# Attention heads: exponentials, normalisation, key scaling and rotary additions issued one or two pumps later

## The reference, cut to what matters

```python
proj = rmsnorm(h) @ w_in                     # q, k, v of the neighbourhood heads; cq, ckv, k_pe of the latent ones
# neighbourhood heads (128 wide): q, k normed per head
s = q @ k.T * scale + bias + mask            # a grid of 64 columns, a window of 16, plus the meta tokens
out_a = softmax(s) @ v
# latent heads (128 + 64 rotary)
q = rmsnorm(cq) @ w_q_up ; k, v = rmsnorm(ckv) @ w_kv_up
q, k = rmsnorm(q), rmsnorm(k) ; rotary on the last 64 columns of each
out_b = softmax(q @ k.T * scale) @ v
h = h + concat(rmsnorm(out_a), rmsnorm(out_b)) @ w_out
h = h + conv_glu(rmsnorm(h))                 # then a second block: recurrence, convolution, gated MLP
```

## Time and profile before

| | |
|---|---|
| median of three runs | 2751.41 us |
| the profiled execution | 2753.61 us |
| its span | 2752.2 us |
| TensorE busy | 2677.2 us (97%), 22052 matmuls |
| VectorE busy | 1836.5 us (67%) |
| ScalarE busy | 1248.1 us (45%) |
| GpSimd busy | 324.8 us (12%) |
| attention of the first block | about 100 to 410 us of the span |

### The profile page before, as it was taken

How to read it: one execution, slowest core, us unless ns; L and a number is a source line. 1 busy time by engine, 2 the same in 40 slices (tenths; PEclk the granted TensorE clock), 3 DMA queues, 4 the chain that set the end, 5 groups by cost and what they waited for, 6 DMA issues and landing times.

```text
span 2752.2 us, 51365 instructions
## 1 busy us (share of the span) xinstructions
PE 2677.2 (97%) x22052; PEld 2636.4 (96%) x22052; DVE 1836.5 (67%) x2578; ACT 1248.1 (45%) x1943; POOL 324.8 (12%) x526
## 2 busy tenths in 40 slices
PE   6999999899999999998999999999989999999998
PEld 6988889899999999998999999999989999999998
DVE  5656568777777777776888667766876445454444
ACT  5556555544433444445434443334544433344443
POOL 1110101111111111221000001111221000000001
PEclk9999999999999999999999999999999999999999
DMA  6433445688888888885444568886767556555553
GB/s 200 120 117 94 125 144 176 202 271 263 271 280 283 268 272 273 266 283 177 142 152 153 185 228 270 276 271 218 256 204 252 184 179 189 193 190 184 184 182 125
DMA packets 500084, 571.22 MB, mean 208 GB/s; under 512 B 26704, under 2 KB 473424, under 8 KB 499856
## 3 DMA queue, kind: packets, MB, share of 16 engines
q1 hardware_dynamic: 467968, 463.76, 51.9%
q0 software_dynamic: 31600, 103.80, 11.6%
q10 hardware_dynamic: 288, 0.36, 0.0%
HBM read 565.77 MB, written 2.54 MB: 206 GB/s over the span
## 4 chain that ended last, share of the span: by engine, by line
PE 86%; DVE 7%; ACT 4%; issue 1%; DMA 0%; POOL 0%; SPq 0%; DVEq 0%; ACTq 0%
PE ps L681 27%; PE ps L682 27%; PE ps L683 26%; DVE wl L1780 3%; ACT wh L1273 2%; PE ps L976 1%; PE ps L810 1%; DVE lr L1976 1%; DVE nx L1884 0%; ACT lp L1446 0%; DMA raw<-in_w_in 0%; PE ps L783 0%; DVE sqt L1884 0%; PE ps L835 0%; PE ps L836 0%
## 5 line engine op out<-in xcount | busy, mean ns | idle before, releaser
L1780 DVE TENSOR_TENSOR wl<-raw,wh 128x1024 fp32r<-128x1024 f32 (+1 forms) x894 | 1058.5, 1200 | 630.4 <-ACT wh L1273 626.2
L681 PE MATMUL ps<-xx,wh 128*128 128x256 f32 (+2 forms) x4848 | 1385.8, 286 | 29.2 <-DVE xx L1861 16.3
L682 PE MATMUL ps<-xx,wh 128*128 128x256 f32 (+2 forms) x4848 | 1366.4, 282 | 0.0
L683 PE MATMUL ps<-xx,wl 128*128 128x256 f32 (+2 forms) x4848 | 1363.1, 281 | 0.0
L1273 ACT ACTIVATE wh<-raw 128x1024 fp32r<-128x1024 f32 (+1 forms) x894 | 882.2, 1029 | 621.8 <-PE ps L683 612.3
L681 PEld LDWEIGHTS ps<-xx,wh 128*128 128x128 f32 x4848 | 918.0, 189 | 38.4 <-DVE wl L1780 21.9
L682 PEld LDWEIGHTS ps<-xx,wh 128*128 128x128 f32 x4848 | 918.9, 190 | 1.7 <-issue 1.0
L683 PEld LDWEIGHTS ps<-xx,wl 128*128 128x128 f32 x4848 | 918.4, 189 | 0.0
L681 PE MATMUL ps<-hid,wh 128*128 128x256 f32 x1408 | 393.9, 280 | 0.0
L682 PE MATMUL ps<-hid,wh 128*128 128x256 f32 x1408 | 393.7, 280 | 0.0
L683 PE MATMUL ps<-hid,wl 128*128 128x256 f32 x1408 | 392.8, 279 | 0.0
(11 more groups left out here) (366 smaller groups left out, 2387.4 us busy)
## 6 DMA issues: line engine op xcount, KB each, us to landing
raw<-in_w_in SPq DMA_DIRECT2D x118, 1024.0 KB, 5.3
ada_raw<-in_w_ada POOLq DMA_DIRECT2D x384, 256.0 KB, 4.7
raw<-in_w_gate SPq DMA_DIRECT2D x44, 1024.0 KB, 6.4
raw<-in_w_up SPq DMA_DIRECT2D x44, 1024.0 KB, 7.0
raw<-in_w_ffn_gate SPq DMA_DIRECT2D x44, 1024.0 KB, 5.1
raw<-in_w_ffn_up SPq DMA_DIRECT2D x44, 1024.0 KB, 5.6
raw<-in_w_down SPq DMA_DIRECT2D x32, 1024.0 KB, 6.6
raw<-in_w_ffn_down SPq DMA_DIRECT2D x32, 1024.0 KB, 5.5
```

What stands on the lines that cost most here:

```text
L681: pe.matmul(dst, h[:, c, o:o + w], x[:, 0, k, g.t0:g.t1], start=(k == 0), stop=False)
L682: pe.matmul(dst, h[:, c, o:o + w], x[:, 1, k, g.t0:g.t1], start=False, stop=False)
L683: m = pe.matmul(dst, l[:, c, o:o + w], x[:, 0, k, g.t0:g.t1], start=False, stop=end)
L1780: dve.tensor_tensor(wl[i % NS][:, part], raw[i % NR][:, part], wh[i % NS][:, part].bitcast(F32), ALU.subtract).then_inc(s_lo, 1)
```

## The change

In every head's generators on ScalarE and VectorE, pauses are moved: the exponential comes one pump later; reciprocal and row scaling come two pumps later for the first two query blocks and one for the last; the reciprocals of the norms and the key scaling come one pump later for the first head of a pair and two for the second; the rotary additions come one pump later. The pauses behind them are shortened by as much, so each generator's length stays. TensorE's and GpSimd's programs are untouched.

```diff
 scalar: attend
+                    yield from pause(1)
                     act.wait_ge(s_ldve[lane], event(DVE_EV, f"mx{j}", n))
                     act.activation(p_, src, ACT.Exp, bias=cc[0:w, 0:1], scale=sc, accum_out=cc[0:w, 1:2]).then_inc(s_lact[lane], 1)
...
-                    yield from pause(PAUSES[1] if j < 2 else PAUSES[2])
+                    yield from pause((PAUSES[1] if j < 2 else PAUSES[2]) - 1)
 vector: attend
+                    yield from pause(2 if j < 2 else 1)
                     dve.wait_ge(s_lact[lane], event(ACT_EV, f"ex{j}", n))
                     dve.reciprocal(cc[0:w, 2:3], cc[0:w, 1:2]).then_inc(s_ldve[lane], 1)
...
-                    yield from pause(PAUSES[1] if j < 2 else PAUSES[2])
+                    yield from pause(PAUSES[1] - 2 if j < 2 else PAUSES[2] - 1)
 vector: rstds
-            def rstds(lane, ACT_EV, n):
+            def rstds(lane, ACT_EV, n, late):
...
+                yield from pause(late)
                 dve.wait_ge(s_lact[lane], event(ACT_EV, "sk", n))
 vector: mla
-                yield from rstds(lane, MLA_ACT, n)
+                yield from rstds(lane, MLA_ACT, n, 1 + j)
...
-                yield from pause(PAUSES[5])
+                yield from pause(PAUSES[5] - j)
...
-                yield from pause(PAUSES[6])
+                yield from pause(PAUSES[6] - 1)
 vector: na
-                yield from rstds(lane, NA_ACT, n)
+                yield from rstds(lane, NA_ACT, n, 1 + j)
...
-                yield from pause(PAUSES[5])
+                yield from pause(PAUSES[5] - 1 - j)
```

## The result

The changed kernel takes 2770.36 us (median of four runs, 2767.63 to 2772.49), the kernel before 2750.01 beside it: a ratio of 1.0071, 95% interval 1.0059 to 1.0083, so 0.7% slower. The forecast was 2769, slower.

A forecast was written before the change was run, and what follows sets the result against it. TensorE, busy 97% of the span, was taken to bound the kernel. Attention terms of 15.7 us plus 1.6 for the clock gave 17.3, moving the median from 2751.41 to 2768.7, stated as 2769; range 2755 to 2780.

The forecast's parts named there:

- L0: First latent head pair: normalisation falls behind the second half's split, so rows reach TensorE's transposes late; +0.85 us.
- N0: First neighbourhood pair: query eviction gap goes, but the second normalisation comes late behind the next slab's split; +0.5 us.
- L1: Second latent pair: key scaling and rotary additions end behind splits, later than TensorE wants them; +1.15 us.
- N1 with L2: Dense stretch of second neighbourhood and third latent pair: keys, rotary products and normalisations late behind splits; +5.0 us.
- N2 with L3: Stretch of third neighbourhood and fourth latent pair: same lateness pattern, VectorE already late at its start; +3.9 us.
- N3: Last neighbourhood pair: second key scaling and second normalisation late behind out projection evictions and splits; +4.3 us.
- For L0 the same chain ends before its transposes: 0: Step claiming the first latent pair's later key scaling and rotary additions still finish before TensorE's transposes; no added time.
- The clock: More and longer TensorE gaps in attention were to bring one more fall of the granted clock; +1.6 us.
- rival C: Each new TensorE gap brings a clock fall, five more at 1.6 us: 2777; chance 0.10.
- A: Rival: with no split delaying normalisation, the spread order closes TensorE's attention gaps, 10 us: 2741, faster; chance 0.08.
- B: Rival: enough slack after all, sums off by a few tenths each and only moves remain: 2751; chance 0.08.
- D: Rival: later exponentials alternate with the other pair's square roots, adding table loads; 2774 with four unhidden; chance 0.04.

The follow-up runs named there:

- e1: The changed kernel with key scaling and rotary additions back at their old pumps, only exponentials, row reciprocals and row scaling late: 2758.75 us, 1.0031 against the kernel before.
- e3: The kernel before with exponential, reciprocal and row scaling all exactly one pump late, keys and rotary additions as before: 2745.91 us, ratio 0.9986.
- e8: e1 with the second half of slabs of more than two chunks split before pump 2 instead of pump 3, during attention: 2750.92 us, 0.9999 against the kernel before.
- e10: e8 with the normalisation of the last neighbourhood pair (N3) one pump late instead of two: 2746.89 us, ratio 0.9991 against the kernel before.
- e2: The changed kernel with softmax back at its old pumps, only key reciprocals, key scaling and rotary additions late: 2766.05 us, ratio 1.0058 against the kernel before.
- e4: The changed kernel with the second half of every slab, two-chunk ones too, split before pump 2: 2764.39 us, ratio 1.0052 against the kernel before.
- e9: The changed kernel with the second half split before pump 2 only in slabs of more than two chunks: 2762.6 us, 1.0041 against the kernel before.
- e6: The changed kernel with GpSimd's mask addition cut from 128x512 to 128x4 elements: 2766.69 us, ratio 1.0055 against the kernel before.
- e5: The changed kernel with the last neighbourhood pair (N3) alone back on its old pumps: 2764.56 us, ratio 1.0053 against the kernel before.
- e7: e3 with the second half split before pump 2 in slabs of more than two chunks: 2749.2 us, ratio 0.9999 against the kernel before.

## Why the prediction was right, and where it was short

**The bound and the place.** Right: all added idle time lies in attention, and the stretches behind are as long as before. Of the signs listed, VectorE's waits for exponentials did not nearly vanish, 6.8 of 17.7 us are left; the others came.

**The mechanism.** Right. For the softmax half (8.2 us, e1) it is shown: not the later exponential but a split ahead of the normalisation makes it late. e3, e8 and e10 each take it away differently and each get the time back. For the keys and rotary additions (15.5 us, e2), the larger half, it is only in part shown: the early split shortens the waits for the rotary product from 10.5 to 6.1 (e4) and 7.5 us (e9), and the rest is read from the timelines, as in the chain at 249.96. Beside it stand GpSimd's collisions (e6) and a clock loss that rests on one profile each.

**The terms**, in us: once as how far the starts of the same TensorE work part between the two profiles, which has clock falls in it, and once as TensorE's waits for attention results in that stretch, after less before:

| step | forecast | starts part by | waits added |
|---|---|---|---|
| L0 | 0.85 | 2.7 | 1.9 |
| N0 | 0.5 | 1.0 | 0.6 |
| L1 | 1.15 | 2.4 | 1.9 |
| N1 with L2 | 5.0 | 6.1 | 4.0 |
| N2 with L3 | 3.9 | 4.1 | 3.6 |
| N3 | 4.3 | 5.8 | 2.9 |
| sum | 15.7 | 22.1 | 14.9 |

The sum without the clock was right within a microsecond, which is partly luck: the latent pairs L0 and L1 were too small (2.0 for 3.8), the large three too large (13.2 for 10.5), and the errors cancel. (By its own figures N3 was 5.9 less 1.4, 4.5 and not 4.3.) From the first sums of squares of L0 to the last product with v the profile grew by 18.9 us (298.65 to 317.54); the 22.1 count from a little later and leave out a clock fall of 3.2 us at 108 to 116 us that the profile before has and the one after has not. It does not come with the change: of the twelve profiles, the three that reach attention last have it (before, e2 and e3). 18.9 less the difference in clock loss, 3.4, is 15.5: the order again. N3 shows how the two stand together: 2.9 us of waits, 3.4 us of clock loss from 392 to 416 us behind them, and undoing N3 alone (e5, whose profile has no loss there) gave 5.8.

**The step that failed** is "For L0 the same chain ends before its transposes: 0". The rotary product ended 1.69 us late, because GpSimd's mask addition fell on two operations of the chain. With L1 this was 2.6 us (e6), where the sum had none. The Trainium skill (SBUF — State Buffer, section "SBUF: two separate sides") had the rule; my estimate by it, 18.4 instead of 17.3, was nearer and still short, because I applied it to L1 only. The trace agrees with the rule: 1.53 us beside GpSimd, 0.42 without. It does not agree in every row with whichever comes second being the one that is blocked: the split of 4.26 us began 0.6 us before the additions that it waited for, by GpSimd's recorded times, which are rough.

**N0.** The eviction gap went and the wait for the normalised row came in its place, 2.58 us for 2.02: the forecast's +0.5. It came sooner than "2 us later" of the text: at 168.72 it is the same transposes that stood at 173.55, in an execution that was about 5 us ahead.

**The clock.** One more fall was forecast. There were more:

```profile
168.00:172.00 4.00, 3.28 (x17) 3.13 (x18) 2.26 (x7) 3.26 (x10) 0.00 (x0) 0.57 0.27 35
```

At 168.72 six transposes took 1.54 us instead of 0.82 at the lower level (1.2 GHz), after a gap of 2.58. Falls in the windows from 252, 332, 392 and 408 followed, 8.5 us in all against 5.1 before. The forecast had 1.6 for it and 3.4 is measured: rival C's mechanism, at less than half its size. The forecast for the profiled execution (2770.9) lies above it (2767.63) and the one for the median (2768.7) below the measured median (2770.36), since the profiled execution was the fastest of four and began its attention 4.9 us earlier than the one before did. That 2769 lies within 1.4 us of the measured median is closer than the terms deserve.

**Rivals.** A and B fall: every pair got new waits, though in L1 only for the rotary product; its normalised rows were in time, as forecast. But A's remark that the spread order closes the eviction and rotary gaps if no split stands between was right, and e3 is that kernel: 2745.9, not 2741, because the normalised rows still wait 3.9 us. D falls by the row of eight loads. The drain that the prediction names beside each load is not seen either: in e8 a load of 1.28 us at 228.52 starts 0.02 us after the copy before it ends, and the exponential at 229.82 starts 0.02 us after the load.

## What to carry to other kernels

On engines that work their queue in order, moving an instruction one step later is judged by what it is now behind, not by the waits it saves: 10.9 us of waits saved on an engine that is not the bound were worth nothing by themselves, and a split of 1.2 us ahead of a result that the bound engine wants was worth 8 us over a stage. Move producer and consumer by the same step, so that nothing comes in between (0.9986), rather than by one and two (1.0031). And when a chain is moved, ask what the other engines do at its new time, in every pair and not only where the old trace showed a collision, and whether a collision that cost nothing until now still has slack to hide in.

## What the runs showed of the hardware

VectorE's operations with two inputs in SBUF outlast GpSimd's addition when they run beside it. Short ones (0.42 us by themselves) end 0.3 us after it: 114.35 + 1.53 against 114.34 + 1.26, and 192.69 + 1.16 against 192.24 + 1.32. A split (1.2 us by itself) ends 1.1 us after it: 378.59 + 4.26 against 379.23 + 2.53. Each ends as if nearly all of its own work were done after the addition. The rotary product at 192.35, with one input in PSUM, ran beside the same addition in its usual 0.41.

The granted clock in attention differs much between kernels that are alike: losses of 1.7 (e7), 3.4 (e3, e8, e10), 5.1 (before), 6.9 (e5), 8.5 (after, e1), 12.0 (e6), 13.7 (e2, e4) and 15.4 us (e9). The four largest all have a gap of 2.9 us or more for the rotary product or the keys, but so have e5 and the changed kernel. That is a correlation over one profile each, not a shown cause.
